# Expert outputs added onto the residual rows in DRAM by accumulating indirect DMAs, with eleven weight slots

## What is computed

```python
x = x + y                                                  # after the token mixer
h = rms_norm(x, norm_ffn_g)
# comb[token, expert]: two non-zero weights a token
act = silu(einsum('bnd,edf->bnef', h, w_g)) * einsum('bnd,edf->bnef', h, w_u)      # e = 32, f = 128
out = einsum('bnef,efd->bnd', act * comb[..., None], w_d)
y   = rms_norm(x + out, norm_final_g)
```

## Time and profile before

| | |
|---|---|
| median of 3 runs | 1412.79 us (1411.11 to 1417.36) |
| the profiled execution | 1414.9 us, span of its trace 1412.9 us |
| PE busy | 1297.0 us, 92% of the span |
| DVE, ACT, POOL busy | 808.7, 386.0, 470.0 us |
| mean granted TensorE clock | 0.957 of full |
| DMA | 163.72 MB, 116 GB/s over the span |

### The profile page before, as it was taken

One profiled execution on the slowest core, in us unless ns is written; L12 is line 12 of the kernel. 1 busy time (PEld: TensorE's weight loads), 2 busy tenths in 40 slices (PEclk: granted clock), 3 DMA queues, 4 the chain that ended last, 5 costly groups with the idle time before them and its releaser, 6 DMA issues.

```text
span 1412.9 us, 20458 instructions
## 1 busy us (share of the span) xinstructions
PE 1297.0 (92%) x7405; PEld 1067.2 (76%) x7405; DVE 808.7 (57%) x2034; ACT 386.0 (27%) x883; POOL 470.0 (33%) x767
## 2 busy tenths in 40 slices
PE   5999999999999999989999999999999849999940
PEld 5988999999989999965556556997555438888830
DVE  5455778889999998736666563342344422222237
ACT  5553222222122123235554342000111111221212
POOL 4801586788851246520000001110111123333314
PEclk9999999999999999999999897999999959999985
DMA  7201332223122311020001223626600069999956
GB/s 244 69 24 42 91 65 73 38 82 80 43 82 80 94 64 31 1 94 1 1 16 32 63 62 128 249 104 219 195 30 31 31 182 289 296 309 298 302 221 277
DMA packets 128427, 163.72 MB, mean 116 GB/s; under 512 B 12498, under 2 KB 104226, under 8 KB 127186
## 3 DMA queue, kind: packets, MB, share of 16 engines
q1 hardware_dynamic: 114273, 129.31, 28.7%
q0 software_dynamic: 12624, 27.62, 6.0%
q10 hardware_dynamic: 1440, 5.58, 1.0%
HBM read 137.80 MB, written 39.21 MB: 125 GB/s over the span
## 4 chain that ended last, share of the span: by engine, by line
PE 85%; POOL 5%; DVE 3%; DMA 2%; ACT 2%; issue 2%; SPq 0%; POOLq 0%; ACTq 0%; DVEq 0%
PE bank L751 10%; PE bank L752 10%; PE bank L753 10%; PE bank L1018 9%; PE bank L1084 8%; PE bank L938 5%; PE bank L902 4%; PE bank L1090 4%; PE bank L925 3%; PE bank L1009 3%; PE bank L1003 2%; PE bank L873 2%; PE bank L1077 2%; PE bank L963 2%; PE bank L1005 2%; PE bank L840 2%
## 5 line engine op out<-in xcount | busy, mean ns | idle before, releaser
L1518 DVE MAX8 small<-region_kv 128x8 f32<-128x272 f32 (+4 forms) x241 | 190.2, 828 | 51.3 <-DVE region_kv L1523 51.2
L751 PE MATMUL bank<-h_hi,w_hi 128*128 128x384 f32 (+1 forms) x576 | 196.1, 340 | 0.0
L752 PE MATMUL bank<-h_lo,w_hi 128*128 128x384 f32 (+1 forms) x576 | 196.1, 340 | 0.0
L1523 DVE MATCH_REPLACE8 region_kv<-small,region_kv 128x272 f32<-128x272 f32 (+4 forms) x241 | 195.5, 818 | 0.0
L753 PE MATMUL bank<-h_hi,w_lo 128*128 128x384 f32 (+1 forms) x576 | 194.4, 338 | 0.0
L751 PE MATMUL bank<-w_hi,h_hi 128*128 128x256 f32 x448 | 129.9, 290 | 1.4 <-ACT region_q L1218 1.4
L1780 POOL TENSOR_TENSOR w_lo<-w_stage,w_hi 128x512 fp32r<-128x512 f32 x64 | 80.8, 1297 | 151.0 <-ACT w_hi L1158 150.8
L1018 PE MATMUL bank<-region_t,region_h 128*128 128x512 f32 x288 | 127.2, 595 | 1.2 <-DVE region_h L1624 1.2
L753 PE MATMUL bank<-w_hi,h_lo 128*128 128x256 f32 x448 | 125.9, 281 | 0.0
L752 PE MATMUL bank<-w_lo,h_hi 128*128 128x256 f32 x448 | 125.8, 281 | 0.0
L753 PEld LDWEIGHTS bank<-h_hi,w_lo 128*128 128x128 f32 x576 | 108.7, 189 | 0.0
(11 more groups left out here) (242 smaller groups left out, 2543.8 us busy)
## 6 DMA issues: line engine op xcount, KB each, us to landing
w_stage<-in_w_in SPq DMA_DIRECT2D x72, 256.0 KB, 3.3
region_kv<-in_xa SPq DMA_DIRECT2D x16, 512.0 KB, 5.5
region_q<-in_wg SPq DMA_DIRECT2D x12, 512.0 KB, 7.0
region_q<-in_wu SPq DMA_DIRECT2D x12, 512.0 KB, 9.2
region_q<-in_wd SPq DMA_DIRECT2D x12, 512.0 KB, 11.2
region_h<-in_wg SPq DMA_DIRECT2D x12, 512.0 KB, 7.3
region_h<-in_wu SPq DMA_DIRECT2D x12, 512.0 KB, 9.6
region_h<-in_wd SPq DMA_DIRECT2D x12, 512.0 KB, 10.9
```

The source lines that it names most:

```text
L751: mm(out, st_hi(k), mv_hi(k), start=(k == 0), stop=False)
L752: mm(out, st_hi(k), mv_lo(k), start=False, stop=False)
L1518: nc.vector.max(m8[:, q, :], x).then_inc(dve_c, 1)
L1523: nc.vector.match_replace(x, m8[:, q, :], x, TAKEN).then_inc(dve_c, 1)
```

## The change

1. `y_d` is gone. In its place stands `sum_d` (`token_sum_scratch`), 1152 rows for the tokens and 128 more. SP stores each residual tile `x2[:, t, :]` there right behind its `h2` tile. In the expert stage POOL issues, for each expert, an indirect DMA with an add (`add_rows`): the 128 rows of `ysb` are added onto the rows of `sum_d` that `gidx` names. Before each but the first, POOL waits until the one before has landed (`y_added`), since two adds onto one row must not overlap.
2. A list entry's code is now the token itself. Gathers use `heads` directly, and `gidx` is min(code, 1152 + partition), so that each unused entry has a row of its own behind the tokens. No row is dropped by bounds: each add moves all 128 rows.
3. At the end SP loads nine tiles of 0.5 MB from `sum_d` over `x2`, and DVE's sums (L1745, L1746) are gone.
4. Three more weight slots lie in the region of `x2`, whose tiles are free once stored: eleven in all. Experts 5 and 6 are loaded within the output projection, 7 when the first gather has landed, 8 to 10 behind it.
5. Gate and up weights are laid out by the host so that each partition's 4 KB are contiguous; all three weight DMAs have rows of 4 KB.

```diff
         eslot = ([RW[:, 0:3072], RW[:, 3072:6144]] + [RQ[:, 3072 * i:3072 * i + 3072] for i in range(3)]
-                 + [RH[:, 3072 * i:3072 * i + 3072] for i in range(3)])
+                 + [RK[:, 3072 * i:3072 * i + 3072] for i in range(3)] + [RH[:, 3072 * i:3072 * i + 3072] for i in range(3)])
...
-        y_d = nc.dram_tensor("expert_rows_scratch", (2 * TOK, D), F32, kind="Internal").ap()
+        sum_d = nc.dram_tensor("token_sum_scratch", (TOK + P, D), F32, kind="Internal").ap()
...
             def load_e(e):
                 s = e % NSLOT
-                sp.dma_start(e_gate(s), a["wg"][e].rearrange("(k p) f -> p k f", p=P)).then_inc(ew_in[s], 16)
-                sp.dma_start(e_up(s), a["wu"][e].rearrange("(k p) f -> p k f", p=P)).then_inc(ew_in[s], 16)
+                sp.dma_start(eslot[s][:, 0:1024], a["wg"][e]).then_inc(ew_in[s], 16)
+                sp.dma_start(eslot[s][:, 1024:2048], a["wu"][e]).then_inc(ew_in[s], 16)
                 sp.dma_start(e_down(s), a["wd"][e]).then_inc(ew_in[s], 16)
+
+            def load_x2_slot(i):
+                for t in range(3 * i, 3 * i + 3):
+                    sp.wait_ge(tile_in[t], 32)
+                load_e(5 + i)
...
                 sp.dma_start(h2_d[t * P:(t + 1) * P, :], h2[:, t % 2, :]).then_inc(h2_out[t % 2], 16)
-            sp.wait_ge(o7_done, 2 * NT)
-            for e in range(5, NSLOT):
-                load_e(e)
+                sp.dma_start(sum_d[t * P:(t + 1) * P, :], x2[:, t, :]).then_inc(tile_in[t], 16)
+                if t in (4, 7):
+                    load_x2_slot((t - 4) // 3)
 
             sp.wait_ge(scattered, 16 * 2 * NT)
             sp.dma_start(heads[:, :, :], lists[0:P, :, :]).then_inc(lidx_in, 16)
+            sp.wait_ge(hg_in[0], 16)
+            load_x2_slot(2)
+            sp.wait_ge(o7_done, 2 * NT)
+            for e in range(8, NSLOT):
+                load_e(e)
...
-            for s in range(3):
-                sp.wait_ge(y_out[s], 16 * ((NE - s + 2) // 3))
+            sp.wait_ge(y_added, 16 * NE)
             sp.wait_ge(over_end, 1)
             for t in range(NT):
-                sp.dma_start(y2[t], y_d[2 * P * t:2 * P * (t + 1), :].rearrange("(p q) d -> p q d", q=2)).then_inc(tile_in[t], 16)
+                sp.dma_start(x2[:, t, :], sum_d[t * P:(t + 1) * P, :]).then_inc(tile_in[t], 16)
...
-                act.wait_ge(y1_done, t + 1)
+                act.wait_ge(tile_in[t], 48)
...
+            link(ts(pad_row, siota, float(TOK), None, ALU.add))
             dve.wait_ge(lidx_in, 16)
-            ts(gidx, heads[:, :, 0], 1, None, ALU.logical_shift_right).then_inc(gidx_ready, 1)
+            ts(gidx, heads[:, :, 0], pad_row, None, ALU.min).then_inc(gidx_ready, 1)
...
                     if y >= 3:
-                        dve.wait_ge(y_out[y % 3], 16 * (y // 3))
+                        dve.wait_ge(y_added, 16 * (y - 2))
...
-            def combine(t):
-                dve.wait_ge(tile_in[t], 32)
-                link(tt(x2[:, t, :], y2[t][:, 0, :], x2[:, t, :], ALU.add))
-                tt(x2[:, t, :], y2[t][:, 1, :], x2[:, t, :], ALU.add).then_inc(y1_done, 1)
...
-            def scatter(src, idx, s):
-                pool.indirect_dma_start(out=y_d, out_offset=bass.IndirectOffsetOnAxis(ap=idx, axis=0), in_=src,
-                                        in_offset=None, bounds_check=2 * TOK - 1, oob_is_err=False).then_inc(s, 16)
+            def add_rows(src, idx, s):
+                pool.indirect_dma_start(out=sum_d, out_offset=bass.IndirectOffsetOnAxis(ap=idx, axis=0), in_=src,
+                                        in_offset=None, compute_op=ALU.add).then_inc(s, 16)
...
+            pool.wait_ge(lidx_in, 16)
+            for e in range(3):
+                gather(hg[:, e, :], heads[:, e, 0:1], hg_in[e])
             pool.wait_ge(gidx_ready, 1)
-            for e in range(3):
-                gather(hg[:, e, :], gidx[:, e:e + 1], hg_in[e])
+            for t in range(NT):
+                pool.wait_ge(tile_in[t], 32)
             for e in range(NE):
                 if e + 3 < NE:
                     pool.wait_ge(te_done, 2 * (e + 1))
-                    gather(hg[:, e % 3, :], gidx[:, e + 3:e + 4], hg_in[e % 3])
+                    gather(hg[:, e % 3, :], heads[:, e + 3, 0:1], hg_in[e % 3])
                 pool.wait_ge(y_ready, e + 1)
-                scatter(ysb[:, e % 3, :], heads[:, e, 0:1], y_out[e % 3])
+                if e >= 1:
+                    pool.wait_ge(y_added, 16 * e)
+                add_rows(ysb[:, e % 3, :], gidx[:, e:e + 1], y_added)
```

More of the change, by code:

```diff
@@ L174, in build @@
         pjunk = sm(3)
+        pad_row = sm(1)
         assert sm_at[0] <= 510
@@ L278, in build @@
         ysb = view(RT, 5632, 3, D)
-        y2 = [view(RW, 2048 * i, 2, D) for i in range(4)] + [view(RT, 8704, 2, D)] + [view(RQ, 2048 * i, 2, D) for i in range(4)]
         gfin = RH[:, 0:1024]
@@ L550, in build @@
         y_ready = sem("y_ready")
-        y_out = sems("y_out", 3)
+        y_added = sem("y_added")
         ov_w = sem("over_weights_in")
@@ L725, in _ @@
             sp.wait_ge(dn_done, NE)
-            sp.dma_start(gfin, a["gfin"]).then_inc(gfin_in, 16)
-            for s in range(3):
-                sp.wait_ge(y_out[s], 16 * ((NE - s + 2) // 3))
+            sp.dma_start(gfin, a["gfin"]).then_inc(g2_in, 16)
+            sp.wait_ge(y_added, 16 * NE)
             sp.wait_ge(over_end, 1)
             for t in range(NT):
-                sp.dma_start(y2[t], y_d[2 * P * t:2 * P * (t + 1), :].rearrange("(p q) d -> p q d", q=2)).then_inc(tile_in[t], 16)
+                sp.dma_start(x2[:, t, :], sum_d[t * P:(t + 1) * P, :]).then_inc(tile_in[t], 16)
             for t in range(NT):
@@ L1726, in _ @@
             dve.wait_ge(over_in, 32)
-            for s in range(3):
-                dve.wait_ge(y_out[s], 16 * ((NE - s + 2) // 3))
+            dve.wait_ge(y_added, 16 * NE)
             n_over = dve.value_load(over_row[0:1, 31:32], min_val=0, max_val=MAX_OVER)
@@ L1751, in final @@
                     op0=ALU.mult, op1=ALU.mult).then_inc(fin_ready, 1)
-            for t in range(NT + 1):
-                if t < NT:
-                    combine(t)
-                if t >= 1:
-                    final(t - 1)
+            for t in range(NT):
+                final(t)
         @block.gpsimd
@@ L1987, in _ @@
                 pool.wait_ge(dn_done, NE)
+                pool.wait_ge(y_added, 16 * NE)
                 with pool.Fori(0, n_over) as it:
@@ L1991, in _ @@
                     row = pool.snap((code // NE) * (P * NE - NE) + code + P * NE, min_val=0, max_val=NE * (TOK - P) + NE - 1)
-                    for dst, src in ((e_gate(0), a["wg"]), (e_up(0), a["wu"])):
-                        pool.dma_start(dst, src[bass.ds(ex, 1), :, :].rearrange("o (k p) f -> p (o k) f", p=P)).then_inc(ov_w, 16)
+                    for o, src in ((0, a["wg"]), (1024, a["wu"])):
+                        pool.dma_start(eslot[0][:, o:o + 1024], src[bass.ds(ex, 1), :, :].rearrange("o p c -> p (o c)")).then_inc(ov_w, 16)
                     pool.dma_start(e_down(0), a["wd"][bass.ds(ex, 1), :, :].rearrange("o p f -> p (o f)")).then_inc(ov_w, 16)
@@ L1999, in _ @@
                     tt(pjunk[:, 0:1], mhalf, mhalf, ALU.add).then_inc(ov_c, 1)
-                    gather(hg[:, 0, :], gidx_o[:, 0:1], ov_h)
+                    gather(hg[:, 0, :], heads_o[:, 0:1], ov_h)
                     pool.wait_ge(y_ready, NE + 1 + it)
                     tt(pjunk[:, 1:2], mhalf, mhalf, ALU.add).then_inc(ov_c, 1)
-                    scatter(ysb[:, 0, :], heads_o[:, 0:1], ov_y)
+                    add_rows(ysb[:, 0, :], gidx_o[:, 0:1], ov_y)
                     pool.wait_ge(ov_y, 16 * it + 16)
@@ L2041, in _constants @@
     entry = np.zeros((P, NT, 2, 2), np.int32)
-    entry[:, :, 0, 0] = 2 * tok
-    entry[:, :, 1, 0] = 2 * tok + 1
+    entry[:, :, 0, 0] = tok
+    entry[:, :, 1, 0] = tok
     return c, b, entry.reshape(P, NT * 4)
```

12 lines of the change are left out of this document (6 added, 6 removed).

## The result

The changed kernel takes **1459.21 us** (median of four runs, 1454.86 to 1461.74), the kernel before beside it 1415.07 (1411.11 to 1417.89): a ratio of 1.0314, 95% interval 1.0295 to 1.0334. The forecast was 1395, its range ended at 1434. The profiled execution took 1461.74 us, its trace 1459.9.

The account below looks back on a forecast made before the run. It took PE to bound the expert stage at 6.24 us an expert, with DMA engines near full, and DVE the end. Hand-over -3.4, stage 0 and end -15.8 sum to -19.2 us: forecast 1395, range 1389 to 1434.

Parts of the forecast that it names:

- I take 0 for the stage: Expert stage: adds land in 5.3 us beside the weights, follow each other within 6.24 us, and cost nothing.
- T: Expert stage: time between successive adds, landing + 0.74 us, or 6.24 if longer; forecast 6.05, under 6.24.
- the low end: Expert stage: reading old rows takes no extra engine time; 5.9 us of engine time an expert, of 6.24.
- the high end: Expert stage: reading old rows costs as much again as writing, 1.3 us; 7.2 us of engine time an expert.
- The company of the weights: Expert stage: weight rows passing between an add's rows lengthen its landing by 0.8 us, from 4.5 to 5.3.
- The turn of the sign at T = 6.86: Expert stage: at add intervals of 6.86 us, a landing of 6.1, the added time equals the 19.2 us gained.
- The first rival: Expert stage: the chain of adds becomes longer than an expert, +10 to +44 us, 1405 to 1439; chance 0.32.
- its extreme: Expert stage: the read comes on top of a 6.9 us landing, T 8.9, +84 us, 1479; chance 0.06 more.
- The hand-over: Router to first expert: shorter last list scatter, 3.0 us, and POOL told directly, 0.4 us; together -3.4 us.
- The end: After the last `ysb`: 35.5 us in place of 51.3, with loads and stores bounding it; -15.8 us.
- The third rival: At the end: POOL's root sets the rhythm, 2.4 us a tile, 39 us for 35.5, 1399; chance 0.12.
- The second rival: Expert stage: weights come late, 203 us of engine time in 200, PE stands some 5 us, 1400; chance 0.07.

Follow-up runs that it names:

- e2: The changed kernel with a plain write in place of the add, still one at a time: 1412.89 us.
- e3: The changed kernel without the 21 weight loads of the expert stage, later experts reusing weights already loaded: 1422.73 us.
- e7: The kernel before with gate and up weights in rows of 4 KB, nothing else: 1411.78 us, ratio 0.9988.
- e12: The changed kernel with adds waiting by expert group, unused rows dropped, used rows spread, overflow table late, gate and up in 512 byte pieces: 1398.29 us, ratio 0.9868.
- e1: The kernel before with one wait more, each scatter waiting until the one before has landed: 1435.14 us.
- e5: The changed kernel with experts of four groups in turn, each add waiting only for the one four places back: 1413.69 us, ratio 0.9990.
- e6: The changed kernel with expert groups in turn, adds waiting by group, and unused rows dropped by a bounds check: 1411.21 us, ratio 0.9978.
- e10: The changed kernel with expert groups in turn, unused rows dropped and used rows spread over the engines: 1396.74 us, ratio 0.9864.
- e4: The changed kernel with a bounds check on the add, so that unused rows are dropped: 1462.57 us.
- e9: The changed kernel with unused rows dropped and used rows spread over all 16 engines: 1432.76 us, ratio 1.0121.

## Why the prediction was wrong

**The step that failed** is the landing of an add, 5.3 us beside the weights, from which "I take 0 for the stage" followed. Measured are 6.2 us alone and 8.3 in the mean of the 19 adds issued while weights were loaded, so that T is 6.9 and 9.0 and not 6.05. Alone it was 4.5 in the sum, 3.2 and 1.3 for the read. The missing 1.7 are 0.6 for POOL's instruction, which I had not priced (1.59 against 1.01 in e2), 0.7 because the 128 added rows hold an engine 2.0 us longer than written ones (3.33 against 1.31) and not 1.3, 0.1 because the lone write of e2 takes 3.3, and 0.3 that stay open. With 0.74 to reissue that is 6.9, already over 6.24 with every other queue empty.

In "I take the low end for engine time, since each byte that a copy reads and writes is already in the 0.16 us" the choice was wrong and the high end about right: an added row takes twice a written one (0.328 against 0.161), and from 1185 to 1335 us, worked out as above, 0.37 against 0.18 in e2. What that high end leaves out are the longer rows, which bring the mean of the quiet stretch to 0.44.

**The company of the weights** was the second mis-sized term of the same step: 0.8 us taken, 2.1 measured (8.3 less 6.2). The 21 later loads alone cost 31 x (8.30 - 7.14) = 36 us over the stage (e3). Even plain writes land in 6.0 us in the median of e2 and up to 9.7, not in 3.3. The earlier trace rows had said so, 6.9 in the median, and I explained it away by the backlog of 512 byte pieces; e7 has 4 KB rows and 7.4.

**The mechanism and its rival** were right in kind. "T = landing + 0.74" holds within 0.1 us (10.78 and 6.91 above). The turn of the sign at T = 6.86 is not shown: e2, at 6.97, should be 3 us slower than the kernel before and was 4 faster, but in its one execution the stage also began 5 us earlier than in the changed kernel. The first rival's way is what happened. Its cases lay at 6.55 to 7.65, its extreme at 8.9 with a chance of 0.06; 8.30 lies between. I gave the row that I had measured too little weight against one that I had reasoned out. The range's upper end, 1434, even left out the rival's own case with the landing of today, 1439.

**Split of the 63.8 us:** the wait alone, with writes, 22.6 (e2); the add on top 41.2. Cut the other way: 28 without the loads (e3), 36 from their company.

**The Trainium skill's rule**, in "Collectives: The Full Stack", section "The bandwidth ceiling: the fold count and why AG ≠ RS ≠ AR", half the rate of a copy for an add, is borne out row by row: 0.328 us against 0.161. It falls short for a whole add of 128 rows, 3.33 us against 1.31, 2.5 times. With the doubled row the first rival had a T of 6.55, and a lone add measures 6.91. The fit in "DMA: Bandwidth & Descriptors", section "Anatomy of one DMA — SWDGE (gpsimd) path", 3.2 us, agrees with the lone write of 0.52 MB (e2, 3.3) and with no added or accompanied one. The prediction set it beside the lone scatter of the earlier trace rows, also 3.2, but that one moves 0.30 MB, for which the fit gives an estimate of 2.7.

**The hand-over** (-3.4): the scatter lands in 2.51 for 5.33, POOL goes from heads to gather in 0.91 for 1.13, the heads take 1.82 for 1.63. That is -2.8. The reason given, that the weights now stand behind, holds: e12 keeps the 512 byte pieces, has the heads ahead and lands it in 2.52. Rows of 4 KB alone do the same in e7 (2.62), because the weights are then through in time. One profile each, at 5.33, e1 at 5.98.

**The end** (-15.8): -14.3 as measured from the last add's issue; the forecast from there was 50.5 to 34.8, measured 36.2, of which 1.7 are the landing. From the load's issue (1429.88) it was 30.0 us where the terms give 30.3. The third rival was right in that POOL's root sets the rhythm in the chain, 2.05 us a tile (1438.17 to 1440.22) and not 2.4; nine tiles of it and the way out come to the same as the transfers that I had summed.

**The second rival** (weights late, 0.07) stayed hidden behind the first and came out in e5 and e6.

**The weight slots and the buffers** did what was said: PE never waited for weights in the changed kernel. The 10 us of buffers were gone after four adds, but "POOL's gather stands ahead of the waiting add and is issued in its shadow, three experts ahead, so it suffers nothing" was wrong: each gather has another add ahead of it, and PE first stood for a gather, 3.05 us before 1196.15. It cost nothing of its own, since the adds set the pace. Nothing was caught up after the loads, as a lone add too is longer than an expert; in e1, with shorter landings once the loads are through, the chain was back on PE.

Open: why a landing beside the loads grows by as much as it does, how an engine divides its time between two queues, and why the first added row on each engine takes so long. No run here changed that alone. Nor is it tested what part the overflow table's trip, moved only on top of e10, has in the late weights of e5.

## What to carry to other kernels

A DMA that waits for the landing of the one before is a chain of landing + reissue (here 0.74 us); compare that with the period of its stage, and take the landing measured under the stage's own traffic, not the idle one. An accumulating DMA is dear in engine time (here two to two and a half copies), so first ask which of them can truly meet: where the data's structure keeps them apart, order the work so that each waits for an old one. Then balance the rows over the engines, since the slowest one decides the landing.

## What was not expected of the hardware

- An added row of 4 KB takes 0.328 us in the median and a written one 0.161 (last add of the changed kernel, last write of e2), but the first added row on each engine takes 0.49 to 1.51. In the mean it is 0.44 us in the quiet stretch and 0.37 from 1185 to 1335 us (41.3% of 150 us for 17 adds with their gathers); a written one in e2 is 0.18 (30.6% of 150 us, worked out the same way).
- The indirect DMA with an add holds POOL 1.59 us, the plain one 1.01, whatever part of its rows is dropped (e4, e9).
- Dropping 44% of the rows hardly shortens the landing (8.5 for 8.8 us beside the loads) unless the used ones are spread over the engines (interval 8.24 to 7.45, 1432.76 us).
- Rows of 4 KB do not make way for another queue: the small list scatter takes 5.6 us amid 4 KB weight rows (e7) and 6.1 amid 512 byte pieces, where 2.3 is the median of its kind, and an expert's scatter takes 7.4 and 6.9. What they change is that the weights are through sooner (411 GB/s for 326, and the earlier trace rows), and no time here by more than 0.3%.
